# A transformer block in fp32: the up projection of the MLP as seven block products per chunk, with three operands read back from DRAM

## The reference, cut to what matters

```python
def rmsnorm(x, g):
    return x * lax.rsqrt(jnp.mean(x * x, axis=-1, keepdims=True) + EPS) * g

u = rmsnorm(h, attn_norm_g)
... # two kinds of attention heads on u @ w_in give oa and ob
h = h + jnp.concatenate([oa, ob], axis=-1) @ w_out
z = rmsnorm(h, mlp_norm_g) @ w_up              # (1024, 1024) @ (1024, 4096)
h = h + jnp.square(jax.nn.relu(z)) @ w_down    # (1024, 4096) @ (4096, 1024)
gate = jax.nn.sigmoid(rmsnorm(h, ple_norm_g) @ w_ple_gate)
h = h + gate * (p @ w_ple_proj)
return rmsnorm(h, final_norm_g)
```

## Time and profile before

| | |
|---|---|
| median of 3 runs | 1266.42 us (1265.95 to 1267.19) |
| profiled execution, first to last instruction | 1264.6 us |
| granted TensorE clock, mean | 0.993 |
| busy: TensorE, VectorE, GpSimd, ScalarE | 98%, 57%, 38%, 34% |
| a chunk, up part and down part | 43.52 and 38.25 us |
| DMA engines, mean share | 21% |

### The profile page before, as it was taken

The page is one execution under the profiler, slowest core; times in us unless marked ns, Lnnn a source line. Parts: engine busy times, 40 slices in busy tenths (PEclk is TensorE's granted clock), DMA queues, the critical chain, the costliest instruction groups (busy, mean ns, idle before and its releaser), DMA issues.

```text
span 1264.6 us, 14755 instructions
## 1 busy us (share of the span) xinstructions
PE 1242.5 (98%) x5921; PEld 992.8 (79%) x5921; DVE 717.0 (57%) x974; ACT 426.6 (34%) x788; POOL 486.1 (38%) x231
## 2 busy tenths in 40 slices
PE   6999999999999999999999999999999999999997
PEld 5777777777677788888888888888888888888886
DVE  5255556566767355856847468376584672453234
ACT  7344435445565442212222122131221221342111
POOL 3221202222426682533524335244253352375643
PEclk8999999999999999999999999999999999999998
DMA  6811101112612231120220311202112012131203
GB/s 223 277 34 34 34 18 34 34 51 51 195 39 67 84 101 66 33 73 30 67 67 1 100 34 50 67 17 91 44 34 83 17 39 62 34 102 53 63 1 133
DMA packets 115258, 83.28 MB, mean 66 GB/s; under 512 B 21673, under 2 KB 103638, under 8 KB 115062
## 3 DMA queue, kind: packets, MB, share of 16 engines
q1 hardware_dynamic: 114806, 81.19, 20.9%
q10 hardware_dynamic: 384, 1.15, 0.2%
HBM read 73.91 MB, written 10.77 MB: 67 GB/s over the span
## 4 chain that ended last, share of the span: by engine, by line
PE 94%; DVE 2%; ACT 1%; issue 1%; DMA 1%; SPq 1%; DVEq 0%; ACTq 0%
PE ps L1146 35%; PE ps L1490 25%; PE ps L1168 23%; PE ps L1278 3%; PE ps L1301 3%; PE ps L1289 1%; PE ps L1365 1%; PE ps L1351 1%; PE ps L1338 1%; ACT e_a L895 1%; PE ps L1211 1%; DMA x_raw<-in_x 1%; PE ps L1182 0%; PE ps L1471 0%; DVE kmax L1777 0%
## 5 line engine op out<-in xcount | busy, mean ns | idle before, releaser
L720 POOL TENSOR_TENSOR w_lo<-w_raw,w_hi 128x1024 fp32r<-128x1024 f32 x63 | 152.7, 2423 | 310.1 <-ACT w_hi L801 310.1
L604 POOL TENSOR_TENSOR w_lo<-w_raw,w_hi 128x1024 fp32r<-128x1024 f32 x40 | 100.0, 2500 | 270.4 <-ACT w_hi L818 270.2
L1146 PE MATMUL ps<-z_hi,w_hi 128*128 128x512 f32 x624 | 193.3, 391 | 0.0
L1146 PE MATMUL ps<-z_hi,w_lo 128*128 128x512 f32 x624 | 192.2, 389 | 0.0
L1146 PE MATMUL ps<-z_lo,w_hi 128*128 128x512 f32 x624 | 192.2, 389 | 0.0
L1168 PE MATMUL ps<-u_hi,w_hi 128*128 128x512 f32 x416 | 177.2, 426 | 2.3 <-DVE o_bt L1719 1.7
L1490 PE MATMUL ps<-x_hi_op,w_hi 128*128 128x512 f32 x456 | 178.4, 391 | 0.0
L1490 PE MATMUL ps<-x_hi_op,w_lo 128*128 128x512 f32 x456 | 177.5, 389 | 0.0
L1490 PE MATMUL ps<-x_lo_op,w_hi 128*128 128x512 f32 x456 | 177.4, 389 | 0.0
L2042 DVE TENSOR_TENSOR h<-ps,h 128x512 f32<-128x512 f32 x224 | 144.8, 683 | 46.2 <-PE ps L1490 44.2
L1168 PE MATMUL ps<-u_hi,w_lo 128*128 128x512 f32 x416 | 164.1, 395 | 0.0
(11 more groups left out here) (182 smaller groups left out, 1680.7 us busy)
## 6 DMA issues: line engine op xcount, KB each, us to landing
w_raw<-in_w_up SPq DMA_DIRECT2D x64, 256.0 KB
w_raw<-in_w_in SPq DMA_DIRECT2D x48, 256.0 KB
w_raw<-in_w_down SPq DMA_DIRECT2D x18, 512.0 KB
raw_a<-in_w_down SPq DMA_DIRECT2D x14, 512.0 KB
x_raw<-in_x SPq DMA_DIRECT2D x8, 512.0 KB, 6.9
h_save<-x_t SPq DMA_DIRECT2D x1, 4096.0 KB, 12.3
h<-h_save SPq DMA_DIRECT2D x4, 1024.0 KB, 10.0
w_raw<-in_w_out SPq DMA_DIRECT2D x16, 256.0 KB
```

The lines of the kernel that those rows point to most:

```text
L604: nc.gpsimd.tensor_tensor(w_lo[:, s * D:(s + 1) * D], w_raw[:, s * D:(s + 1) * D], w_hi[:, s * D:(s + 1) * D].bitcast(F32), ALU.subtract). ...
L720: nc.gpsimd.tensor_tensor(w_lo[:, s * D:(s + 1) * D], raw, w_hi[:, s * D:(s + 1) * D].bitcast(F32), ALU.subtract).then_inc(lo_done, 1)
L1146: mm = nc.tensor.matmul(o[i], w, xx[:, x0[i]], start=(first and n == 0), stop=(last and n == 2))
```

## The change

The up part of each chunk becomes seven block products too: the 512 x 1024 tokens and the 1024 features are halved, an operand `xu[n]` is 512 features (four tiles of 128) by 512 tokens, and product n takes 2 x 4 x 3 = 24 matmuls (`up_product`). The operands are the same seven combinations, here of the normalised `h`, made once before and during chunk 0: ScalarE applies the gain, VectorE takes differences and rests (`gained_with`, `turn_rest`, `turns`). Seven operands of 16 KB a partition don't fit beside the rest, so those of B11, B21 and T1 are saved to DRAM (`keep`) and their space is used by the down part's operands; SP reads all three back in each chunk (`give_back`, 2 MB each). The up weights are combined like the down weights (`up_s1` to `up_s4`).

In PSUM, pair 6 holds product 0, then takes products 4, 5 and 6 on top; pair 0 holds product 2 and takes product 3 on top; pair 4 holds product 1. Between them ScalarE copies product 0 (`keep_m1`), product 2 (`keep_m5`) and the sum after product 4 (`keep_u2`) to SBUF, and VectorE adds the other banks to these (`add_kept`). `positive` then takes max(z, 0) * rstd, with `rstd` now to the power -0.5, and ScalarE squares the result in place. The differences go to tiles of their own (`combine`).

The diff, cut (TensorE first, then ScalarE, VectorE, GpSimd, SP):

```diff
+            def up_product(c, n):
+                b, op = up_block(c, n), UP[n]
+                pe.wait_ge(lo_done, b + 1)
+                if c and n < 3:
+                    pe.wait_ge(xu_back[n], 16 * c)
+                for i in range(2):
...
+                    elif n == 3:
+                        pe.wait_ge(m5_ok, 2 * c + i + 1)
+                    elif n == 4:
+                        pe.wait_ge(m1_ok, 2 * c + i + 1)
+                    elif n == 5:
+                        pe.wait_ge(u2_ok, 2 * c + i + 1)
+                    elif n == 6:
+                        pe.wait_ge(c_add, 6 * c + 4 + i + 1)
+                    for k in range(4):
...
+                        mm = step(bank(UP_BANK[n] + i), k * 2 * P + i * P, b % 2, xu_hi[op][:, kc], xu_lo[op][:, kc],
+                                  n < 3 and k == 0, k == 3, n >= 3)
+                    mm.then_inc(blk_done if i else u_tile, 1)
...
             for c in range(CHUNKS):
-                for i in range(4):
...
-                    wblock(up_block(c, i), up_pair(c, i), z_hi, z_lo)
+                up_product(c, 0)
+                if c == 0:
+                    sums(1, 2)
+                up_product(c, 1)
+                up_product(c, 2)
+                if c == 0:
+                    spread(2, 2)
+                for n in range(3, 7):
+                    up_product(c, n)
                 if c < CHUNKS - 1:
                     for n in range(7):
                         products(c, n)
...
+            turns_hi(2)
+            act.wait_ge(s_pool, 2)
+            raw_hi(up_block(0, 3), first_a12[:, :])
+            turns_hi(3)
+            turn4_hi(3)
+            take_rstd(2, 2)
             for c in range(CHUNKS):
...
+                keep_m5(c, 0)
...
+                for i in range(2):
+                    keep_u2(c, i)
+                act.wait_ge(a22_full, 16 * (2 * c + 1))
+                raw_hi(up_block(c, 6), up_a22(c)[:, :])
+                for i in range(2):
+                    square_block(c, C12, i)
...
+                    round_turn(c, T1, 0)
+                slot_hi(product(c, 0), 0, 2 * c + 2)
+                for i in range(2):
+                    square_block(c, C22, i)
+                round_block(c, B22, C22)
...
+                round_turn(c, T3, 2)
+                round_turn(c, T2, 4)
+                act.wait_ge(s_dve, 4 * c + 3)
+                raw_hi(product(c, 1), s_sum[:, :])
+                for i in range(2):
+                    square_block(c, C21, i)
+                round_block(c, B21, C21)
+                round_turn(c, T4, 6)
+                act.wait_ge(s_pool, 4 * c + 3)
+                raw_hi(product(c, 2), slot[0])
...
-            token_norm(2, 5)
+            turns(0)
+            up_s1(0)
+            turns(1)
+            dve.wait_ge(stat, 1)
+            mean_square(2, ps[:, 2 * 512:2 * 512 + TT])
+            turns(2)
+            diagonals(2)
+            up_s3(0)
+            turns(3)
+            turn4(3)
+            turn4_rest(3)
...
+            for c in range(CHUNKS):
...
+                for i in range(2):
+                    add_kept(c, C12, i)
+                    positive(c, C12, i)
+                if not last:
+                    for i in range(2):
+                        squared(c, C12, i)
+                        combine(x_op[T1][:, half_of(i)], c12[:, half_of(i)], c11[:, half_of(i)], ALU.subtract)
+                add_kept(c, C22, 0)
+                positive(c, C22, 0)
+                if not last:
+                    rest(c, T1, x_op[T1])
+                add_kept(c, C22, 1)
+                positive(c, C22, 1)
...
+                for i in range(2):
+                    squared(c, C22, i)
+                    combine(x_op[T3][:, half_of(i)], c22[:, half_of(i)], c12[:, half_of(i)], ALU.subtract)
+                for i in range(2):
+                    dve.wait_ge(t_ok, 8 * c + 2 + i + 1)
+                    combine(x_op[T2][:, half_of(i)], x_op[T3][:, half_of(i)], c11[:, half_of(i)], ALU.add)
+                down_s1(c)
+                for i in range(2):
+                    positive(c, C21, i)
+                for i in range(2):
+                    squared(c, C21, i)
+                    dve.wait_ge(t_ok, 8 * c + 4 + i + 1)
+                    combine(x_op[T4][:, half_of(i)], c21[:, half_of(i)], x_op[T2][:, half_of(i)], ALU.subtract)
+                rest(c, T2, x_op[T2])
+                rest(c, B22, c22)
+                down_s3(c)
+                gather(c, 0)
+                rest(c, T3, x_op[T3])
+                rest(c, B21, c21)
+                dve.wait_ge(t_ok, 8 * c + 8)
+                rest(c, T4, x_op[T4])
+                for n in range(1, 6):
                     gather(c, n)
+                up_s1(c + 1)
+                gather(c, 6)
...
             for c in range(CHUNKS):
...
+                if c:
+                    raw_lo(up_block(c, 0), slot[0])
+                    up_s2(c)
+                    raw_lo(up_block(c, 1), up_a12(c)[:, :])
+                    up_s4(c)
+                    raw_lo(up_block(c, 2), s_sum[:, :])
...
+                raw_lo(up_block(c, 6), up_a22(c)[:, :])
...
                 raw_lo(product(c, 0), slot[0])
-                pool.wait_ge(s_dve, 2 * c + 1)
+                pool.wait_ge(s_dve, 4 * c + 3)
...
+                sp.wait_ge(blk_done, product(c, 1) + 1 - DONE0)
+                give_back(0)
...
+                load_up(raw_a12[:, :], a12_full, c + 1, 1, 0)
+                sp.wait_ge(blk_done, product(c, 5) + 1 - DONE0)
+                give_back(2)
```

More of the change, by code:

```diff
@@ L60 @@
 PRODUCTS = (B11, T1, T2, B22, T3, T4, B21)
+HI_TURN = {B11: 0, T1: 1, B22: 2, T3: 3, T2: 4, B21: 5, T4: 6}
+LO_TURN = {B11: 0, T1: 1, T2: 2, B22: 3, T3: 4, B21: 5, T4: 6}
+LAST_TURN = {B11: 0, B12: 1, B22: 2, B21: 3}
+UP = (B11, B21, T1, B22, T2, T3, T4)
+UP_BANK = (6, 4, 0, 0, 6, 6, 6)
+C11, C12, C22, C21 = range(4)
+LAST_IN = 2 * CHUNKS
 Y_DVE, Y_ACT = (2, 3, 4, 5, 6, 7), (0, 1)
@@ L558, in _ @@
+            sp.wait_ge(xu_ok, first_turn(T1, 3))
+            keep(0)
+            keep(2)
+            sp.wait_ge(lo_done, MLP0)
+            load_up(raw1, r_in[1], 0, 0, 1)
+            sp.wait_ge(job_done, done("O7", 1))
+            load_up(first_a22[:, :], a22_full, 0, 1, 1)
+            sp.wait_ge(xu_ok, first_turn(B21, 3))
+            keep(1)
+            for c in range(CHUNKS - 1):
+                sp.wait_ge(lo_done, up_block(c, 3) + 1)
                 if c == 0:
                     sp.wait_ge(sq_ok, 2 * DT + 1)
-                    load_part(raw_a12[:, :], a12_full, c, 1, 0)
@@ new lines, in _ @@
+                give_back(1)
+                sp.wait_ge(lo_done, product(c, 5) + 1)
+                load_up(raw_a22[:, :], a22_full, c + 1, 1, 1)
+                sp.wait_ge(lo_done, product(c, 6) + 1)
+                load_up(raw_a12[:, :], a12_full, c + 1, 1, 0)
+                sp.wait_ge(blk_done, product(c, 5) + 1 - DONE0)
+                give_back(2)
+            c = CHUNKS - 1
+            sp.wait_ge(s_dve, 4 * c + 2)
+            sp.wait_ge(s_pool, 4 * c + 2)
+            for n in range(4):
+                sp.wait_ge(lo_done, up_block(c, 4 + n) + 1 if n < 2 else product(c, n - 2) + 1)
+                rows = wdown_v[:, 4 * c:4 * c + 4, 2 * n * P:2 * (n + 1) * P]
+                sp.dma_start(w_raw[:, (n % 2) * D:(n % 2 + 1) * D].rearrange("p (k m) -> p k m", m=2 * P), rows
+                             ).then_inc(r_in[n % 2], 16)
@@ new lines, in _ @@
+            for k in range(2):
+                act.wait_ge(job_done, done("O7", 1))
+                gained_second(k)
+            turns_hi(0)
+            gained_second(2)
+            for i in range(2):
+                keep_m1(0, i)
+            act.wait_ge(s_dve, 1)
+            raw_hi(up_block(0, 2), s_sum[:, :])
+            turns_hi(1)
+            gained_second(3)
+            turns_hi(2)
+            act.wait_ge(s_pool, 2)
+            raw_hi(up_block(0, 3), first_a12[:, :])
+            turns_hi(3)
@@ L1051, in _ @@
-                if c == CHUNKS - 1:
+                        keep_m1(c, i)
+                    act.wait_ge(s_dve, 4 * c + 1)
+                    raw_hi(up_block(c, 2), s_sum[:, :])
+                    square_block(c, C11, 0)
+                    act.wait_ge(s_pool, 4 * c + 2)
+                    raw_hi(up_block(c, 3), raw_a12[:, :])
+                    square_block(c, C11, 1)
+                keep_m5(c, 0)
+                if c and not last:
+                    round_block(c, B11, C11)
+                keep_m5(c, 1)
@@ L2008, in last_operands, with up_s1 @@
-            def last_operands(i):
-                kk, first = i // 2, LAST + 2 * i
-                own = temp[i % 2]
-                pair = (B11, B12) if i % 2 == 0 else (B21, B22)
-                for half, n in enumerate(pair):
-                    rest(first + half + 1, n, kk, own[:, half_of(half)])
+            def up_s1(c):
+                if c:
+                    dve.wait_ge(lo_done, product(c - 1, 3) + 1)
```

(20 more changed lines are left out.)

593 lines of the change are left out of this document (365 added, 228 removed).

## The result

The changed kernel takes 1312.13 us (1311.22 to 1313.3) where the kernel before takes 1266.18 on the same chip: a ratio of 1.0364, 95% interval 1.0352 to 1.0376. It is slower by 46 us; the forecast was 1301, its range 1272 to 1320. The profiled execution's span is 1311.5 us, 46.9 above that of before, where the sum had said 35.0.

A forecast was written before the change was run, and what follows sets the result against it. TensorE, busy 98% of the span, was taken to bound the kernel. Terms 0.8 + 19.7 + 2.0 + 17.6 - 5.1 = +35.0 on the span 1264.6 gave 1299.6, with 1.8 for the median 1301 us; range 1272 to 1320.

The forecast's parts named there:

- Direction and mechanism: Head of the down part: VectorE and GpSimd exclude each other on the SBUF port, so the chunk grows and time rises.
- The walk of a steady chunk: Chunks 1 to 6: 8.55 us of waits on 76.16, so 84.7 us against 81.77, +17.6 in all.
- D3's 0.6: Down product D3 of a steady chunk: starts 0.6 us late because D1's first gather ends at 62.9, not 62.34.
- the clock: Chunk 0: its 8 us hole brings the half clock once, some ten matmuls at 0.22 more, +2 us.
- the fall at D2 in every chunk: Rival: the hole before D2 halves the clock in every chunk, 1.8 us more seven times, 1314 us; chance 0.15.
- the likeliest case: Port serialises VectorE and GpSimd at the head of the down part, chunk grows: 1290 to 1308 us; chance 0.50.
- Chunk 0: First chunk: waits of 3.0 at U2, 8.1 at the spread and 5.9 at U3; 105.1 against 85.4, +19.7 us.
- Out blocks: Just before chunk 0: four VectorE and ScalarE round trips creep by 0.75 a block, +0.8 us (0 to 2).
- last chunk: No differences or second weight set: 5.44 us less, up to 0.3 wait for the B12 rests, -5.1 us.
- transfers: Read backs of 6 MB a chunk, some 6 us for each 2 MB, stay hidden and add nothing.
- The rival of S3 before S4: VectorE's weight sum S3 gets the port before GpSimd's S4: 2.26 us less in seven chunks, 1285; chance 0.14.
- The faster case: Waits not where put, covers hold: D2 at most 5.4 us late, about 1230 with no waits; chance 0.16.

The follow-up runs named there:

- Experiment 1: Changed kernel with five GpSimd instructions at the head of the down part replaced by memsets of about their length: 1256.57 us, ratio 0.9921.
- experiment 4: Changed kernel with two of D1's four tiles multiplied twice, 12 matmuls more in a chunk, to keep TensorE working before D2: 1311.53 us.
- experiment 5: Changed kernel with chunk 0 alone reordered: mean square, diagonals, GpSimd's root, and ScalarE's rstd and U2 copy go earlier: 1308.4 us, ratio 1.0329.
- experiments 3: Changed kernel with VectorE's list reordered: each gather goes ahead of the rests that the next product doesn't need: 1274.23 us, ratio 1.0059.
- experiment 8: Changed kernel with gathers ahead of later rests, chunk 0 reordered, and weight sum S2 moved from GpSimd to VectorE behind S1: 1262.35 us, ratio 0.9967.

## Why the prediction was right, and where it was not

**Direction and mechanism: right, and shown.** TensorE has 5.44 us a chunk less to do and is kept waiting for more than that where the down part begins, since VectorE and GpSimd exclude each other. Experiment 1 takes away the reads of one side and nothing else of its load, and 55.6 us go, more than the whole loss.

**The walk of a steady chunk: right to 0.25 us for each wait but the last.** Predicted 0.7, 2.0, 1.55 and 3.7 for U6, its second half, D1 and D2; measured 0.95, 1.78, 1.43 and 3.59. D3's 0.6 didn't show, since TensorE was itself late by then. Sum 7.75, predicted 8.55.

**The step that failed: the clock, which the sum took in chunk 0 alone.** The forecast gave the fall at D2 in every chunk to a rival, with 0.15, on the ground that holes of 1.3 us show none. The hole of 3.6 us shows it seven times. The rival's price was "eight or so matmuls" and 1.8 us; the slow matmuls lost 1.7 us in four of the six chunks and 3.0 in two. 76.2 + 7.75 + 1.7 or 3.0 is 85.6 or 86.9, measured 86.0 and 87.3 (the rest is in gaps under 0.3 us each). The mean of 86.45 is 1.75 above the 84.7 forecast: 2.1 for the clock and 0.4 for the gaps, less 0.8 for the waits. In six chunks that is 10.5 of the 11.9 us that the span lies above the sum. The rival's 1314 was nearer to the 1312.1 than the forecast's 1301; the likeliest case's own range, 1290 to 1308, missed. "TensorE: Matmul & The Clock Gate", HAM oscillation, in the Trainium skill describes the pattern, a wait in each pass that brings back 1.2 GHz each time, and the rows agree: clock 0.50 for three to six us after each D2 wait. What it cost net, 1.3 us a chunk by the reading under experiment 4 and 1.5 in the one chunk under experiment 5, was not isolated by a run of its own.

A row that bears on this chance was misread besides. The prediction takes for a fall after TensorE had waited 7.28 us, but that is the length of a transfer. TensorE's own pauses there were 1.22, 1.96 and 0.19 us, with transposes between them, and the granted clock was 1.00 until 15 us and 0.50 from 16 us on:

```profile
11.43 1.09 PE L1227 MATMUL ps<-ident,x_raw 128*128 128x128 f32 x8 [1.22 <-DMA x_raw<-in_x]
14.48 1.09 PE L1227 MATMUL ps<-ident,x_raw 128*128 128x128 f32 x8 [1.96 <-DMA x_raw<-in_x]
```

So the trace of before held a fall after pauses shorter than the 3.7 us that the walk put before D2.

**Chunk 0: the total right by luck, its parts not.** D2 of chunk 0 was predicted 79.3 us after the start of the MLP (105.1 less the 27.8 us behind D2, and 2 for the clock) and came at 547.08 - 467.9 = 79.2. But the waits are 2.89, 4.12 and 6.46 where 3.0, 8.1 and 5.9 stood: 3.5 less. The spread was not so late: the diagonals end at 493.15, 25.3 after the last out block, walked as 29.1. The half clock gave it back. The chain in order of time shows what follows the first hole, the second hole, and what follows that:

```profile
493.19 3.78 PE ps L1418 x4
496.97 6.30 issue
503.27 14.07 PE ps L1720 x48
```

Four spread matmuls take 3.78 us, today 1.72, and the 48 after the second hole 14.07, where 48 take 10.88: 5.3 us, predicted 2. The 3.5 us too much in the waits and the 3.3 too little for the clock cancel.

**Out blocks, last chunk, transfers.** The MLP starts at 467.9, 0.8 later, as the sum had it. From the last D2 wait on, the span is 1.5 us over the sum. The transfers are hidden, as predicted, but take 8.3 us each and not 6.

**The rival of S3 before S4** did not happen: at 801.95 the same GpSimd instruction goes in ahead of S3. **The faster case** asked for D2 no more than 5.4 us late; D2 came 7.75 late in all, the waits at U6 and D1 counted. But it hung on the lists' order: experiments 3 and 8 take back 38 and 50 us with the same arithmetic. What experiment 8 leaves, 2.75 us of waits at U6, some 1 in small gaps and D3's, and chunk 0, is why seven products win only 4 us where 43.5 us of matmuls went.
